# Heads of two attention groups in a mixed order, with projection tiles, rotations and key stores to match

## What is computed

```python
h = x + 0.5 * swiglu(rmsnorm(x, g_ffn1), w1g, w1u, w1d)
u = rmsnorm(h, g_mix)
qa, ka, va, qb, kb, vb = split(u @ w_in)        # then rotary positions on q and k
oa = swa_prompt(qa, ka, va, sinks)              # A: 8 query heads, 2 key heads, window of chunks, sinks
ob = diff_prompt(qb, kb, vb, lam)               # B: 4 heads, each two maps: p0 - lam * p1, whole past
ob = rmsnorm(ob, g_subln) * (1.0 - lam_init)
h = h + concatenate([oa, ob]) @ w_out
h = h + 0.5 * swiglu(rmsnorm(h, g_ffn2), w2g, w2u, w2d)
```

## Time and profile before

| | |
|---|---|
| three runs | 1094.17, 1096.92, 1097.12 us; median 1096.92 |
| profiled execution | 1096.9 us, span of its instructions 1095.0 us |
| TensorE matmuls busy | 1070.8 us (98%) |
| VectorE busy | 692.8 us (63%) |
| ScalarE busy | 474.6 us (43%) |
| POOL busy | 86.5 us (8%) |
| mean granted TensorE clock | 0.991 |
| chain that ended last | TensorE 90%, VectorE 6%, ScalarE 2%, issue 2% |

### The profile page before, as it was taken

One profiled execution on the slowest core, in us unless ns is written; L12 is line 12 of the kernel. 1 busy time (PEld: TensorE's weight loads), 2 busy tenths in 40 slices (PEclk: granted clock), 3 DMA queues, 4 the chain that ended last, 5 costly groups with the idle time before them and its releaser, 6 DMA issues.

```text
span 1095.0 us, 19038 instructions
## 1 busy us (share of the span) xinstructions
PE 1070.8 (98%) x7890; PEld 1041.0 (95%) x7890; DVE 692.8 (63%) x1083; ACT 474.6 (43%) x817; POOL 86.5 (8%) x84
## 2 busy tenths in 40 slices
PE   9999999999999999988999999999999999999996
PEld 9999999999999999977788889999999999999996
DVE  6898732488883333476677766699863268886323
ACT  6536631256653223333334444554652136665222
POOL 0000000000000114021322102200000000000112
PEclk9999999999999999998999999999999999999998
DMA  5232232232213225220112212232222323232202
GB/s 205 78 120 112 62 99 92 81 113 84 110 56 104 73 74 190 78 72 1 49 49 68 73 39 71 66 135 81 101 81 81 106 78 114 78 104 80 80 28 87
DMA packets 22660, 94.43 MB, mean 86 GB/s; under 512 B 2928, under 2 KB 6000, under 8 KB 18096
## 3 DMA queue, kind: packets, MB, share of 16 engines
q1 hardware_dynamic: 22576, 93.23, 25.2%
HBM read 88.24 MB, written 4.98 MB: 85 GB/s over the span
## 4 chain that ended last, share of the span: by engine, by line
PE 90%; DVE 6%; ACT 2%; issue 2%; DMA 0%; POOL 0%; SPq 0%; DVEq 0%; ACTq 0%; POOLq 0%
PE acc L673 46%; PE acc L755 34%; PE acc L893 3%; PE acc L981 1%; PE acc L994 1%; DVE ssq L1738 1%; PE acc L951 1%; DVE sq L1740 0%; PE acc L929 0%; DMA raw<-in_w1gu 0%; DVE st L1787 0%; PE acc L919 0%; ACT h_hi L1153 0%; DVE ssq L1541 0%; DVE st L1794 0%
## 5 line engine op out<-in xcount | busy, mean ns | idle before, releaser
L1471 DVE TENSOR_TENSOR w_lo<-raw,w_hi 128x1024 fp32r<-128x1024 f32 (+3 forms) x145 | 176.3, 1217 | 210.5 <-ACT w_hi L1099 210.1
L755 PE MATMUL acc<-c_hi,w_lo 128*128 128x288 f32 x952 | 282.0, 296 | 0.0
L755 PE MATMUL acc<-c_hi,w_hi 128*128 128x288 f32 x952 | 280.9, 295 | 0.0
L755 PE MATMUL acc<-c_lo,w_hi 128*128 128x288 f32 x952 | 277.6, 292 | 0.0
L673 PE MATMUL acc<-h_hi,w_hi 128*128 128x288 f32 x1024 | 222.1, 296 | 0.0
L673 PE MATMUL acc<-h_lo,w_hi 128*128 128x288 f32 x1024 | 221.1, 295 | 0.0
L673 PE MATMUL acc<-h_hi,w_lo 128*128 128x288 f32 x1024 | 221.0, 295 | 0.0
L1099 ACT ACTIVATE w_hi<-raw 128x1024 fp32r<-128x1024 f32 (+3 forms) x145 | 149.1, 1028 | 165.3 <-PE acc L673 146.9
L755 PEld LDWEIGHTS acc<-c_lo,w_hi 128*128 128x128 f32 x952 | 180.8, 190 | 0.0
L755 PEld LDWEIGHTS acc<-c_hi,w_hi 128*128 128x128 f32 x952 | 179.0, 188 | 0.0
L755 PEld LDWEIGHTS acc<-c_hi,w_lo 128*128 128x128 f32 x952 | 178.5, 187 | 0.0
(11 more groups left out here) (207 smaller groups left out, 1299.0 us busy)
## 6 DMA issues: line engine op xcount, KB each, us to landing
raw<-in_w1gu SPq DMA_DIRECT2D x17, 1024.0 KB, 4.8
raw<-in_w2gu SPq DMA_DIRECT2D x17, 1024.0 KB, 4.8
raw<-in_w1d SPq DMA_DIRECT2D x16, 704.0 KB, 4.0
raw<-in_w2d SPq DMA_DIRECT2D x16, 704.0 KB, 4.1
raw<-in_w_qk SPq DMA_DIRECT2D x13, 512.0 KB, 3.6
raw<-in_w1gu SPq DMA_DIRECT2D x10, 512.0 KB, 4.5
raw<-in_w2gu SPq DMA_DIRECT2D x10, 512.0 KB, 3.8
raw<-in_w_out SPq DMA_DIRECT2D x8, 512.0 KB, 3.9
```

What stands on the lines that cost most here:

```text
L755: m = nc.tensor.matmul(acc[:, banks[side(f)], 0:HALF], w_part[:, col:col + P], x_part[:, k, c, :], start=n in (P1, P5, P2) and k == 0 and ...
L1471: return nc.vector.tensor_tensor(cols, src, hi.bitcast(FP32), ALU.subtract).then_inc(split_ready, 1)
```

## The change

The heads come in the order A0 A1 B0 A2 B1 A3 B2 B3, and the tiles in an order in which each head's tiles come ahead of it. Weight blocks are put into memory in the order of `TILES`. `step` gets a second condition: the last step of a tile is put into the list only when the scores that must free the slots of the tile before are in it. All tables of numbers are other ones; of them one line is shown here. The scores of A0.0 and A0.1 and the normalisation of A0.0 change places at the start.

```diff
-TILES = ["ka", "qa0", "qa1", "qa2", "qa3"] + [f"{n}b{h}" for h in range(B_HEADS) for n in "kq"]
+TILES = ["ka", "qa0", "qa1", "kb0", "qb0", "qa2", "kb1", "qb1", "qa3", "kb2", "qb2", "kb3", "qb3"]
+UNIT_ORDER = ("A0", "A1", "B0", "A2", "B1", "A3", "B2", "B3")
...
-FILL_START = (3, 3)
+FILL_START = (2, 4)
...
-    for t in range(PAIRS):
-        units += [("A", t, 0), ("A", t, 1), ("As", t, 0)]
-    for h in range(B_HEADS):
-        units += [("Bs", h, 0)] + [("B", h, i) for i in range(SEQ_TILES)] + [("L", h, 0)]
+    for kind, t in UNIT_ORDER:
+        t = int(t)
+        if kind == "A":
+            units += [("A", t, 0), ("A", t, 1), ("As", t, 0)]
+        else:
+            units += [("Bs", t, 0)] + [("B", t, i) for i in range(SEQ_TILES)] + [("L", t, 0)]
     events, done = [], [0]
+
+    def free_slots(b):
+
+        name = TILES[b]
+        former = [c for c in range(b) if TILES[c][:2] == name[:2] and int(TILES[c][2]) % 2 == int(name[2]) % 2]
+        beside = [c for c in range(b) if name[0] == "q" and TILES[c][0] == "q" and c % 2 == b % 2]
+        return {n for n, (kind, t, _) in enumerate(units) for c in former + beside
+                if kind != "L" and kind[0].lower() == TILES[c][1] and t == int(TILES[c][2])
+                and (c in former or kind[1:] == "s")}
...
+        b, k = FILLERS[done[0]]
+        if FIRST_TILES < b < len(TILES) and k == KD - 1 and not free_slots(b - 1) <= {e[1] for e in events if e[0] == "S"}:
+            return False
...
     score(0)
     fill(FILL_START[0])
+    events.append(("N", 0))
     score(1)
-    events.append(("N", 0))
     fill(FILL_START[1])
```

More of the change, by code:

```diff
@@ L2104, in head_cols @@
         return np.concatenate([w[:, h * HEAD + HEAD_ORDER] for h in heads], axis=1)
-    groups = [head_cols(wka, (0, 1))] + [head_cols(wqa, (t, t + PAIRS)) for t in range(PAIRS)]
+    groups = {"ka": head_cols(wka, (0, 1))}
+    for t in range(PAIRS):
+        groups[f"qa{t}"] = head_cols(wqa, (t, t + PAIRS))
     for h in range(B_HEADS):
-        groups += [head_cols(wkb, (2 * h, 2 * h + 1)), head_cols(wqb, (2 * h, 2 * h + 1))]
-    w_qk = np.concatenate([tiled(g, P) for g in groups], axis=0)
+        groups[f"kb{h}"] = head_cols(wkb, (2 * h, 2 * h + 1))
+        groups[f"qb{h}"] = head_cols(wqb, (2 * h, 2 * h + 1))
+    w_qk = np.concatenate([tiled(groups[name], P) for name in TILES], axis=0)
     w_v = np.concatenate([wva, wvb], axis=1)
```

14 lines of the change are left out of this document (7 added, 7 removed).

## The result

The changed kernel takes 1098.15 us in the median of 16 runs (1096.48 to 1101.23), the kernel before 1096.78 us beside it (16 runs, 1090.86 to 1098.59). The ratio is 1.0029, with a 95% interval of 1.0015 to 1.0043. The forecast was a small gain, 1095.5 us. The profiled execution of the changed kernel took 1098.07 us with a span of 1096.2 us and a mean granted clock of 0.992; that of before took 1096.9 us.

The account below looks back on a forecast made before the run. It took TensorE as the bound in the middle stage, with at most 20 us to be had from idle time, clock and switches. Terms +0.8 -1.2 -1.85 -3.4 +1.7 +1.7 +0 +0.9 = -1.35 from 1096.9 gave 1095.5 us, range 1090.5 to 1101.5.

Parts of the forecast that it names:

- 1. start: Before kb0's first step: VectorE waits for ScalarE's exponentials, gap some 3.4 us, +0.8 us; the low clock behind it stays.
- 2. first A tiles: Behind kb0's last step: the 1.34 us wait goes, 0.72 before A1.0's product becomes 0.9; -1.2 us.
- 3. A1 to the next head: At the product of A1's cached keys: the 2.15 us wait goes, 0.3 at qa2 come; -1.85 us.
- 3. clock at 508 us: The low clock from 508 to 515 us goes with the 2.15 us wait; -3.4 us.
- 4. late tiles: Waits for VectorE's takes from kb1 to oa3: sum 7.0 us where the old order had 5.4; +1.7 us.
- 4. clock behind kb3: The wait of about 2 us before kb3's first step brings the clock down, a shorter drop; +1.7 us.
- 5. the end: Before the last head is turned back: the 1.55 us wait and the low clock behind it stay; 0.
- 6. switches: 63 runs of projection steps between attention work instead of 54, each costing 0.1 us beyond its steps; +0.9 us.
- 7. queues: SyncE's weight loads behind waiting key stores come no later; nothing gained, nothing lost; 0.
- A rule beside the rows: Normalisation just behind a VectorE take, beside POOL's rotation, costs 1 to 2 us more; sum would be 1094.5, left out.
- The faster one: Rival, chance 0.30: VectorE keeps up at the late tiles, half of their 7.0 us goes, clock stays up; 1090.3 us.
- The slower one: Rival, chance 0.22: VectorE late at A3.0's maxima through POOL contention, kb3's wait passes 3 us; 1101.7 us.

Follow-up runs that it names:

- norm_behind_take: Changed kernel with old start, third query-diagonal slot and early last-head norm, plus A2.0's normalisation behind VectorE's take of qb1: 1092.66 us, ratio 0.9973 to the kernel before.
- three_slots: Changed kernel with three slots of block-diagonal queries instead of two: 1097.39 us, ratio 1.0036 to the kernel before.
- before_new_start: Kernel before with only the start's exchange, A0.0's normalisation ahead of A0.1's maxima on VectorE: 1098.49 us, ratio 1.0046.
- before_norm_early: Kernel before with its last head's normalisation right behind its output product, fillers behind it: 1094.80 us, ratio 0.9993.

## Why the prediction failed

Each term against the two profiled executions, in us of waits unless said otherwise.

| place | forecast | measured |
|---|---|---|
| 1. start | +0.8 | 2.35 to 3.39: +1.04 |
| 1. clock at the start | 0 | low behind it in both: -0.28 |
| 2. first A tiles | -1.2 | 1.34 and 0.72 to 0.82: -1.24 |
| 3. A1 to the next head | -1.85 | 2.15 to 0.24 + 0.24 + 0.37: -1.30 |
| 3. clock at 508 us | -3.4 | gone: -3.03 (one profile only) |
| 4. late tiles | +1.7 | 5.32 to 8.61: +3.29 |
| 4. clock behind kb3 | +1.7 | behind qa3: +1.52 |
| 5. the end | 0 | wait 1.55 again: 0; the clock stayed up |
| 6. switches | +0.9 | +1.16 |
| 7. queues | 0 | 0: no load among the releasers |
| sum | -1.35 | +1.16 |

**The step that failed is place 4**, the sum of the late tiles, by 1.6 us of the 2.5 between -1.35 and +1.16. Its largest terms were right: kb3 2.12 for 2.0, qb1 1.18 for 1.15, oa2 1.08 for 1.15, oa3 0.50 for 0.45, kb1 0.36 for 0.3. Wrong was qa3, sized 1.0 and measured 2.15. I had put only "A2.1's maxima just ahead" there. But the normalisation of A2.0 stands ahead of these maxima, and it waits for exponentials:

```profile
534.40 1.22 DVE L1486 TENSOR_TENSOR w_lo<-raw,w_hi 128x1024 fp32r<-128x1024 f32 x1
536.58 0.16 DVE L1831 TENSOR_TENSOR st<-st 128x4 f32<-128x4 f32 x1 [0.96 <-ACT probs L1348]
...
538.24 0.27 DVE L1796 MEMSET acc<- 64x256 f32 x1
...
540.54 0.79 DVE L1753 STREAM_SHUFFLE ssq<-acc 128x576 f32<-128x576 f32 x1
```

It is the pattern of the start, which I had worked out in place 1 and did not look for again. With that normalisation moved away (norm_behind_take) the wait at qa3 fell by 1.04 us.

A second cause stands earlier in the same chain, and I had left it out of the sum ("A rule beside the rows"). The normalisation of B0.3 runs just behind kb1's take, beside POOL, in the changed kernel:

```profile
528.72 1.11 DVE L1840 TENSOR_TENSOR st<-st,lam 128x1 f32<-128x1 f32 x1
...
530.27 1.65 DVE L1843 SCALAR_TENSOR_TENSOR probs<-probs,st 128x512 f32<-128x512 f32 x1
531.97 0.27 DVE L1796 MEMSET acc<- 64x256 f32 x1
```

The same two take 0.16 and 0.75 us at 579 us, where POOL is idle. The scores of A2.0 had ended at 530.92, so its maxima, begun at 531.97, and all behind them up to the take could have come up to 1.05 us earlier. That it counts is seen in three_slots, where the first of the two was 0.36 us shorter and so was the wait. Each of the two causes comes near the 1.15 us that were missing; no run removes both.

The rest of the miss in this place is small waits that I had left out or sized low (qb2 0.35 for 0.1, oa1 0.47), less 0.45 at qb3 (0.40 for 0.85): POOL was held, its q_diag addition idle for 6.70 us and released by As3's scores, and it cost less than I had counted.

**Place 3** missed two small waits (+0.55). The forecast of 0.3 at qa2 held (0.24), but the product of As1 still waited 0.24 and the scores of Bs0 0.37 for POOL's q_diag.

**Place 1** was right to 0.01 us in the gap itself (some 3.4, measured 3.39), and "the low clock behind it stays" held: in the old order with the old start the clock fell there in all three profiles that have the two waits, and in the new one it fell behind 3.39 us. **The clock of place 3** is another matter. The 3.4 us that I booked as a sure gain at 508 us are a gain only against executions that lose them. Of the three profiles of the old order with a wait of 2.15 us there the clock fell in one, the profile that I read. The size was off too: half of the time at the low clock was booked, and it costs 0.44 of it. Without the falls the two profiled executions are 2.95 us apart, 1.79 in waits and 1.16 in the rest; what the clock takes off or puts on top of that differs from run to run.

**The rivals.** The faster one did not come: VectorE was caught at each late tile. The slower one asked for a wait of over 3 us at kb3 and got 2.12, with the clock at 1.00 behind it in that profile; the changed kernel came out slower all the same, by a wait at qa3 that I had put at 1.0. The contention with POOL that this rival named was there, ahead of qa3 and not of kb3. Three signs by which I had said I would see it wrong, a short gap before kb0, late waits under 4 or over 10 us, a weight load as releaser, did not show either: they would have caught other errors than the one made. Of the signs for the forecast, the gap before kb0, the 2 us at kb3 and POOL's hold came; the idle time was 15.2 us instead of 13 to 14, and the clock fell at qa3 instead of kb3.

**What remains open.** How often the clock falls behind a wait of 1.3 to 2.9 us was only seen, not put under control; the numbers of runs at each level differ from chip to chip. How the miss at qa3 divides between VectorE's idle time and its contention with POOL is open too. The price of a switch rests on one kernel with ten more; in the mixed order it comes out between 0.09 and 0.22 us.

## What to carry to other kernels

Where an in-order engine has two pieces of work and one of them waits for another engine, look at every place in the program where that pair occurs, not only where the diff shows it; the piece that can run at once goes ahead, and a consumer of both pieces pays the difference in full. Before an element-wise piece is moved to just behind an instruction that wakes another engine on the same memory, read what the same instruction takes there: here a move worth 1.0 us cost 2.0 in contention, and two other moves lost 0.9 to 1.8 us in the same way. Take the clock from many runs, not from one profile: a wait that dropped it in every profile is a loss to count on, one that drops it in some is worth only a part, and two middle waits were cheaper than one long one. When work is compared between profiles with different falls of the clock, charge a fall only for the time in which the engine ran, at the price read from the rows: half of every low stretch would put the rest of before at 208.2 us and that of before_new_start at 207.5, though both do the same work in the same number of runs, and the price read from the rows puts them at 208.97 and 209.09.

## What was not expected of the hardware

The granted clock falls after waits of 1.4 to 2.2 us in some executions and not in others of the same kernel. In the changed kernel's profile it fell behind 2.15 us (0.74 over the next 6.5 us) and stayed at 1.00 behind 2.12 us at kb3; in before's it fell behind 2.15 and 1.55 us and stayed up behind 1.62. At qa3 it fell behind 2.15, 2.12 and 2.12 us in three profiles and stayed up behind 2.12 in a fourth and behind 1.78 and 1.79 in three more; at kb3 it fell in two profiles and stayed up in five, each with 2.11 to 2.13 us. At waits of 2.93, 3.39 and 4.73 us it fell in each of the eight profiles that have one, in six of them before the wait had ended (0.61 us before in the changed kernel's). Outside the stage the same holds at the start of the program: a wait for VectorE near 22 us measured from 0.55 to 1.43 us in these profiles. In the five where it was 1.43 the clock was down behind it, as in the changed kernel's:

```profile
26.00:30.00 4.00, 4.00 (x22) 3.79 (x22) 0.52 (x1) 0.54 (x1) 0.00 (x0) 0.77 0.48 172
```

In one more (before_norm_early) it was down there behind 0.55 us, and in the others, with up to 1.32 us, it stayed up, so the length of that wait alone doesn't decide it.

So runs of one program lie on levels about 1.6 us apart, and a change of 1 us can be seen only when it adds or removes a wait that decides between them, or when quickest runs with the same mean clock are set side by side.
